# Gate tiles of a PEER layer: element scatters for two token tiles, one-hot products for the third, and each picked expert's U and V row fetched in one gather

## The reference, cut to what matters

```python
idx = jnp.take_along_axis(cand_i, pos, axis=-1)           # 8 heads x 16 experts a token
gates = jax.nn.softmax(top_s, axis=-1)
u = expert_u[ib]
act = jax.nn.gelu(jnp.einsum('td,thkd->thk', hb, u), approximate=False)
vv = expert_v[ib]
return jnp.einsum('thk,thkd->td', gb * act, vv)
```

## Time and the profile before

| | us |
|---|---|
| median of three runs | 1579.27 |
| runs | 1577.04 to 1581.59 |
| the profiled execution, its time | 1581.45 |
| its span | 1579.1 |
| PE busy | 1542.4 |
| DVE busy | 1263.5 |
| ACT busy | 717.6 |
| POOL busy | 343.5 |

### The profile page before, as it was taken

One profiled execution on the slowest core, in us unless ns is written; L12 is line 12 of the kernel. 1 busy time (PEld: TensorE's weight loads), 2 busy tenths in 40 slices (PEclk: granted clock), 3 DMA queues, 4 the chain that ended last, 5 costly groups with the idle time before them and its releaser, 6 DMA issues.

```text
span 1579.1 us, 23361 instructions
## 1 busy us (share of the span) xinstructions
PE 1542.4 (98%) x8161; PEld 1362.7 (86%) x8161; DVE 1263.5 (80%) x2625; ACT 717.6 (45%) x1128; POOL 343.5 (22%) x305
## 2 busy tenths in 40 slices
PE   7999998999999999999999999999999999999997
PEld 5786666789999999999999999988888888888886
DVE  6775655478988998898999999567888888888886
ACT  5424754443434343343667676434333333333333
POOL 0000003104122222222122222122333333333300
PEclk8999999999999999999999999999999999999999
DMA  9691021046878878789698998999999999999982
GB/s 361 237 366 64 1 107 57 0 174 259 286 247 283 294 235 277 252 291 295 230 319 299 339 321 300 355 326 319 361 348 356 355 351 361 348 360 351 353 284 103
DMA packets 177139, 427.38 MB, mean 271 GB/s; under 512 B 15072, under 2 KB 99200, under 8 KB 172416
## 3 DMA queue, kind: packets, MB, share of 16 engines
q1 hardware_dynamic: 140160, 291.67, 52.4%
q0 software_dynamic: 36864, 134.23, 24.2%
HBM read 373.42 MB, written 52.43 MB: 270 GB/s over the span
## 4 chain that ended last, share of the span: by engine, by line
PE 76%; DVE 1%; DMA 1%; ACT 0%; issue 0%; DVEq 0%; ACTq 0%
PE ps_y L1941 11%; PE ps_y L1945 11%; PE ps_y L1943 11%; PE ps_u L1153 11%; PE ps_u L1155 11%; PE ps_u L1154 11%; PE ps_g L1644 5%; PE ps_q L1320 2%; PE ps_q L1322 2%; PE ps_q L1321 2%; PE ps_s L1332 1%; DMA activations<-u_act 1%; PE ps_u L1976 0%; DVE y_scaled L1887 0%; DVE row L1908 0%
## 5 line engine op out<-in xcount | busy, mean ns | idle before, releaser
L1153 PE MATMUL ps_u<-h_hi,u_hi 128*128 128x384 f32 x1024 | 349.0, 341 | 1.2 <-ACT u_act L1163 0.9
L1155 PE MATMUL ps_u<-h_hi,u_lo 128*128 128x384 f32 x1024 | 344.9, 337 | 0.0
L1154 PE MATMUL ps_u<-h_lo,u_hi 128*128 128x384 f32 x1024 | 344.7, 337 | 0.0
L1812 ACT CAST v_hi<-v_raw 128x1024 fp32r<-128x1024 f32 x128 | 134.7, 1052 | 326.1 <-issue 320.9
L1212 POOL DMA_INDIRECT row<-in_v,row_index x128 | 173.2, 1353 | 376.7 <-DVE h_row L1232 320.4
L1212 POOL DMA_INDIRECT row<-in_u_rows,row_index x128 | 145.9, 1140 | 491.4 <-DVE row_dots L1219 404.7
L1870 DVE TENSOR_TENSOR v_lo<-v_raw,v_hi 128x1024 fp32r<-128x1024 f32 x128 | 160.4, 1253 | 101.3 <-ACT v_hi L1812 101.3
L1941 PE MATMUL ps_y<-v_hi,w_hi 128*128 128x512 f32 x768 | 237.9, 390 | 0.3 <-DVE w_lo L1857 0.3
L1945 PE MATMUL ps_y<-v_hi,w_lo 128*128 128x512 f32 x768 | 237.1, 389 | 0.0
L1943 PE MATMUL ps_y<-v_lo,w_hi 128*128 128x512 f32 x768 | 237.0, 389 | 0.0
L1143 DVE TENSOR_TENSOR u_lo<-u_raw,u_hi 128x1024 fp32r<-128x1024 f32 x128 | 155.0, 1217 | 69.3 <-ACT u_hi L1136 69.3
(11 more groups left out here) (302 smaller groups left out, 2236.0 us busy)
## 6 DMA issues: line engine op xcount, KB each, us to landing
u_raw<-in_u SPq DMA_DIRECT2D x128, 512.0 KB, 5.0
v_raw<-in_v SPq DMA_DIRECT2D x128, 512.0 KB, 5.7
activations<-u_act SPq DMA_DIRECT2D x128, 192.0 KB, 5.2
gate_tiles<-g_tile SPq DMA_DIRECT2D x12, 2048.0 KB, 9.1
gates<-gate_tiles SPq DMA_DIRECT2D x32, 768.0 KB, 8.2
act<-activations SPq DMA_DIRECT2D x128, 192.0 KB, 6.3
w_ada<-in_w_ada SPq DMA_DIRECT2D x23, 1024.0 KB, 7.7
w_proj<-in_w_proj SPq DMA_DIRECT2D x16, 512.0 KB, 4.7
```

What stands on the lines that cost most here:

```text
L1153: pe.matmul(out, self.hi[n][:, k], hi, start=(k == 0), stop=False)
L1154: pe.matmul(out, self.hi[n][:, k], lo, start=False, stop=False)
L1155: last = pe.matmul(out, self.lo[n][:, k], hi, start=False, stop=(k == KD - 1))
```

## The change

- `stick_breaking` also fills the part of `g_dram` of two dense tiles (8 tiles of 32 tokens, 16.8 MB) with zeros: four DMAs from one zeroed tile `blank`. `gated_linear` waits for them at its end.
- `mixer_back`: the eight `w_lo` go from POOL to DVE.
- `retrieval`: for the first two dense tiles ("loose") DVE works out, for each pick, its address in `g_dram` (`places_of`, `columns_of`, `jumps_of`, `cells_of`). As one expert can be picked by two heads, the gates of equal picks in earlier heads are added (`equal_picks`, `equal_gates`, `equal_sums`, `owe`: three operations over 512 g elements for head g, in turn g+1; `board` lies over the old `hits`). POOL then writes 32 scatters a head, each 128 elements of 4 bytes, 256 in all, at a pace written as block numbers (`SPREAD_AT`, `SPREAD_PACE`). Head 7's are prepared in `dense_gates`.
- `dense_gates`: one-hot products for the third tile alone, 16 batches, 37 blocks among them; three transposes for nine, and `product(80)` ahead of them.
- rows: one table of 2048 values (U row, V row), 128 gathers of 1 MB into a ring of four, for 256 of 0.5 MB into a ring of eight. For each pick dot, then Gelu and weight on ACT (one column each), and at the next pick the add. `ROW_PACE` spreads them: 30 by block 80, 68 by block 128 (61 by block 120), 128 by step 120 of V.
- `experts`: SP waits for all scatters before the first load of gates; two of the four activation buffers are now `up.act[0:2]`, so two loads come later.

```diff
+LOOSE_TILES = 2
+SPREADS = LOOSE_TILES * TOPK
-DOTS_BY = [0, 0, 8, 20, 32, 44, 56, 68, 81]
+ROW_PACE = [(16, 0), (80, 30), (128, 68), (248, PICKS)]
+SPREAD_AT, SPREAD_PACE = 13, 11.5
+def rows_by(b):
+    for (b0, n0), (b1, n1) in zip(ROW_PACE, ROW_PACE[1:]):
+        if b < b1:
+            return n0 + max(0, b - b0) * (n1 - n0) // (b1 - b0)
+    return PICKS
...
+            part = LOOSE * N_EXPERTS // P // FILLS
+            sp.wait_ge(blank_done, 1)
+            for n in range(FILLS):
+                sp.dma_start(flat[:, n * part:(n + 1) * part].rearrange("p (a n) -> p a n", n=D),
+                             blank[:].rearrange("p (o n) -> p o n", o=1).broadcast_to([P, part // D, D])).then_inc(keep["filled"], 16)
...
-                pool.tensor_tensor(w_lo[n % WS][:], keep["w_out"][:, n], w_hi[n % WS][:].bitcast(F32), ALU.subtract).then_inc(wlo, 1)
+                dve.tensor_tensor(w_lo[n % WS][:], keep["w_out"][:, n], w_hi[n % WS][:].bitcast(F32), ALU.subtract).then_inc(wlo, 1)
...
-    RING = 8
+    RING = 4
...
+    def weigh(self, act, q):
+        act.wait_ge(self.dotted, q + 1)
+        act.activation(self.act[:, q:q + 1], self.dots[:, q:q + 1], ACT.Gelu).then_inc(self.acted, 1)
+        act.wait_ge(self.acted, q + 1)
+        act.wait_ge(self.gated, q // TOPK + 1)
+        act.activation(self.weight[:, q:q + 1], self.act[:, q:q + 1], ACT.Identity, scale=self.gate[:, q:q + 1]).then_inc(self.weighed, 1)
+    def vector_at(self, dve, b, h_row):
+        for q in range(rows_by(b), rows_by(b + 1)):
+            self.dot(dve, q, h_row)
+            if q > 0:
+                self.add(dve, q - 1)
...
+    def equal_picks(self, dve, g, board):
+        mine = self.expert[:, 0:LOOSE_TILES, self.own(g)].rearrange("p b (k o) -> p b k o", o=1)                   .broadcast_to([P, LOOSE_TILES, TOPK, g * TOPK])
+        return dve.tensor_tensor(self.twin(g, board), mine, self.earlier(self.expert[:, 0:LOOSE_TILES], g), ALU.is_equal)
+    def equal_gates(self, dve, g, board):
+        return dve.tensor_tensor(self.twin(g, board), self.twin(g, board), self.earlier(self.gate[:, 1:1 + LOOSE_TILES], g), ALU.mult)
+    def equal_sums(self, dve, g, board):
+        return dve.tensor_reduce(self.twins[:], self.twin(g, board), AX.X, ALU.add)
...
+            q = 0
+            for g in range(PEER_HEADS):
+                for n in range(SPREADS):
+                    while q < PICKS and gather_at(q) < SPREAD_AT + SPREAD_PACE * (g + n / SPREADS):
+                        rows.gather(pool, q)
+                        q += 1
+                    spread_gate(pool, g, n)
...
+        def spread_gate(pool, g, n):
+            b, j = n // TOPK, g * TOPK + n % TOPK
+            if n == 0:
+                pool.wait_ge(picks.summed, g + 1)
+                if g > 0:
+                    pool.wait_ge(spread, 16 * SPREADS * g)
+            pool.indirect_dma_start(out=g_dram, out_offset=bass.IndirectOffsetOnAxis(ap=picks.cell[:, b, j:j + 1], axis=0),
+                                    in_=picks.owed[:, b, j:j + 1], in_offset=None).then_inc(spread, 16)
...
-        N_BATCH = DENSE // BATCH
+        N_BATCH = P // BATCH
...
+                    rows.vector_at(dve, b, h_row)
+                if x < PER_TILE:
+                    late_gates(2 * x)
+                    late_gates(2 * x + 1)
+                if x == PER_TILE - 1:
+                    dve.sem_inc(picks.summed, 1)
         def tensor(pe):
+            up.product(pe, FIRST)
             pe.wait_ge(chain, 4)
...
+            sp.wait_ge(spread, 16 * SPREADS * PEER_HEADS)
             load_gates(0)
```

More of the change, by code:

```diff
@@ L56 @@
 PICKS = PEER_HEADS * TOPK
+G_TOK = 32
+G_CELLS = N_EXPERTS * G_TOK
 ROW_TOK = P
@@ L1235, in retrieval @@
-def retrieval(nc, life, io, keep, picks, up, rows, h_row, query):
+        u = self.row[n][:, 0]
+        dve.tensor_tensor_reduce(u, u, h_row[:], 1.0, 0.0, ALU.mult, ALU.add, self.dots[:, q:q + 1]).then_inc(self.dotted, 1)
+    def weigh(self, act, q):
[4 more added lines that the diff above has]
+        act.activation(self.weight[:, q:q + 1], self.act[:, q:q + 1], ACT.Identity, scale=self.gate[:, q:q + 1]).then_inc(self.weighed, 1)
@@ L1239, in retrieval @@
+def retrieval(nc, life, io, keep, picks, up, rows, h_row, query, g_dram, spread):
     with ExitStack() as ctx:
@@ L1422, in beside @@
                         up.vector_at(dve, done[0])
+                        if done[0] == ROW_BLOCK[0]:
+                            dve.wait_ge(h_kept, 2)
+                        rows.vector_at(dve, done[0], h_row)
                         done[0] += 1
-                    while done[1] < DOTS_BY[h] + int(share * dots):
-                        if done[1] == 0:
-                            dve.wait_ge(h_kept, 2)
-                        rows.dot(dve, done[1], h_row)
-                        done[1] += 1
                 def settle(share):
@@ L1723, in experts @@
         over = lambda n: ctx.enter_context(nc.sbuf_tensor(n, [P, D], F32, side="right"))[:]
-        gate2, g_fin, squared = over("gate2_rows"), over("g_final_rows"), over("row_squares")
-        y_row, y_pair = h_row[:], [over(f"y_scaled{n}") for n in range(2)]
+        gate2, g_fin = over("gate2_rows"), over("g_final_rows")
+        y_row, squared, y_pair = rows.y[:], rows.row[0][:, 1], [rows.row[n][:, 1] for n in (1, 2)]
         total, rstd = sb("square_sums", [P, TB]), sb("rstd_rows", [P, TB])
@@ L1798, in sync @@
                 sp.wait_ge(o_done, b + 1)
-                sp.dma_start(io["out"][b], out_row[b][:]).then_inc(stored, 16)
+                sp.dma_start(io["out"][b], out_row[b]).then_inc(stored, 16)
             sp.wait_ge(stored, 16 * TB)
         def gpsimd(pool):
-            for r in range(PICKS + rows.RING, ROWS):
-                rows.gather(pool, r)
+            pass
         def scalar(act):
@@ L1832, in squares @@
                 act.activation(rstd[:, b:b + 1], total[:, b:b + 1], ACT.Exp, scale=-0.5).then_inc(rstd_done, 1)
-            act.wait_ge(rows.row_used, PICKS)
-            act.activation(rows.weight[:], rows.dots[:], ACT.Gelu).then_inc(rows.acted, 1)
             for i in range(-OPENING, N_KEYS):
@@ L1919, in vector @@
                     weigh(i + 2)
-                for r in adds_at(i):
-                    rows.add(dve, r, y_row)
+                rows.vector_at(dve, N_KEYS + i, h_row)
+                if N_KEYS + i == ROW_BLOCK[PICKS - 1] + 2:
+                    rows.add(dve, PICKS - 1)
                 if block_ok(i + 2):
```

313 lines of the change are left out of this document (197 added, 116 removed).

## The result

| | before | after |
|---|---|---|
| median, us (4 runs each) | 1579.53 | 1600.73 |
| range | 1577.04 to 1581.59 | 1598.53 to 1604.36 |
| span of the profiled execution | 1579.1 | 1596.7 |

The ratio is 1.0137, 95% interval 1.0110 to 1.0164: 1.4% slower, where 1531 (1515 to 1555) was forecast. In runs 4 and 5 two and one of the executions took over 1.5% longer than the fastest of the same kernel, and they are told apart there.

What follows compares the result with a forecast made beforehand. PE was taken to bound the kernel, with DVE the runner-up. Savings of 46.7 and 0.9 us, together 47.6, took the profiled 1581.45 to 1533.9; that execution lying 2.2 over the median, the forecast was 1531, range 1515 to 1555.

Steps and rivals of the forecast that it cites:

- What PE saves: Dense_gates: 32 of 48 one-hot batches go at 1.78 us, 57.0 us; fewer transposes, and the present wait and slow clock go.
- What DVE gets: Retrieval and dense_gates: equal-pick operations at 0.15 us + 1.04 ns an element; PE late by 14.7, leaving 46.7 us less.
- the signs: Expected marks of the new profile, among them a largest equal-pick operation of 3.7 us and PE waits of about 15 us.
- What feeds it: Retrieval and dense_gates: POOL instructions 1.24 us apart need 50.8 of 56.7 us; DMA share sums to 0.92.
- Rival 2: Late gathers: POOL falls behind, DVE waits for rows in dense_gates; some 10 us in each of two groups, 1551; chance 0.20.
- The two later activation loads: V stage: the loads have some 8 us to spare, so their cost is zero.
- Rival 3: Retrieval and dense_gates, blocks 13 to 105: scatter packets fill the DMA engines; +225 us, 1757, at 176 ns a packet; chance 0.10.
- The rule weighed with it: Scatters in retrieval and dense_gates: small writes done as read-modify-write, 19 us a turn, 40 us over the kernel, 1571.
- The mixer: Moving `w_lo` from POOL to DVE: 0.9 us less, with bounds of -3 (no clock drop) and +2.
- The fill: Stretch from 130 to 220 us: writing 16.8 MB of zeros costs zero, 0 to 5 us if stores are far slower.

Runs made afterwards that it cites:

- run 4: Changed kernel with no picked rows due in blocks 118 to 129: three executions from 1600.08 to 1607.14 us, two of 1627.52 and 1636.46.
- run 5: Changed kernel without the three wide operations on equal picks a head: three executions from 1612.76 to 1625.47 us, one of 1643.39.
- run 1: Changed kernel with one scatter in eight (32 of 256, the rest left out): 1548.40 us.
- run 12: Changed kernel with its 256 scatters turned into gathers (reads) of the same elements, low parts as in the changed kernel: 1593.28 us.
- run 3: Changed kernel with one loose tile instead of two (128 scatters, 32 batches of one-hot products): 1572.71 us.
- run 6: Changed kernel with one loose tile and no picked rows due in blocks 118 to 129: 1562.76 us.
- run 8: Changed kernel with low parts made by a one-input operation (raw x 0) instead of the two-input subtraction: 1643.68 us, a single execution.
- run 9: The kernel of run 8 with its 256 scatters turned into gathers (reads) of the same elements: 1565.92 us, two executions.
- run 13: Changed kernel with one loose tile (128 scatters) and low parts made by a one-input operation: 1561.48 us.
- run 2: Changed kernel with all 256 scatters, each of 16 partitions instead of 128: 1658.41 us.
- run 7: Changed kernel with a semaphore for each loose tile, so a head's first scatter waits only for the same tile's previous head: 1615.97 us.
- run 18: The kernel of run 17 with 26 rows instead of 30 by block 80 and 52 instead of 60 by block 118: 1570.73 us.
- run 17: Changed kernel with scatters paced over 13 blocks a head, no rows due in blocks 118 to 129, a semaphore for each loose tile: 1552.11 us.
- run 10: Changed kernel with the scatters' schedule started 5 blocks later (18 for 13), same pace: 1614.19 us.

## Why the prediction was wrong

By its own steps:

- **What PE saves** was right, as far as the runs show: a batch still takes 1.78 us. Run 1, the nearest to the change without its scatters, has 1548.4, and without the border's 11.6 it is within 6 of the forecast.
- **What DVE gets** was right in price: the largest equal-pick operations take 3.95 and 3.89 us for a forecast of 3.88 (0.15 + 3584 x 1.04 ns), and 12.3 us of waits where 14.7 were forecast, in the run in which POOL is out of the way. (The 3.7 among the signs does not follow from that sum.)
- **What feeds it** is the step that failed, in the term for POOL: "50.8 at 1.24, but 67.8 at the V gathers' mean of 1.35 + 0.3 ... I take 1.24, as scatters move few bytes." The 1.24 of the earlier trace rows are two gathers with DVE out of the way. Measured is 1.65, so 41 of them take 67.6 us where 56.7 are to be had: the upper bound of the sum, 67.8, was the right value. That the two agree so closely is luck, as the bound has 1.35 busy and 0.3 of issue, and the measured 1.65 is 1.27, 0.29 and 0.09 at the heads' borders, a wait that the sum left out. An instruction of POOL hardly depends on bytes (0.97 us for 128 elements of 4 bytes, 0.99 for a row gather of 1 MB). It is held while DVE works through operations of two inputs in SBUF, up to 8.44 us, and the value that the forecast chose has no room for it. The earlier trace rows had shown the two engines in each other's way, and it was used for the mixer only.
- **Rival 2** was the case that came. Its price failed as well: "some 10 us in each of two groups" supposes that POOL catches up. It can't while it is asked for 68 in 57: each head adds 11, and each gather waits behind them. Runs 12 and 1 put it at 45 us (1593.3 less 1548.4), with whatever 224 reads of 128 elements cost besides.
- **The two later activation loads** had "some 8 us to spare: zero". The border cost 11.2 us of PE (10 by runs 3 and 6). The room was counted for loads alone; the gate store, SP's wait and the stores behind it, all beside rows at 0.8 MB a block, use it up.
- **Rival 3**, packets that fill the DMA engines, did not come: from 687 to 950 us the DMA share is 0.74, for 0.87 in the same window of the kernel before. The sum had a packet for each element, 28 x 128 a turn (3584, not 3560) at 46 ns, a share of 0.19. The trace has sixteen packets a scatter, 448 a turn, at 13 ns, and sixteen more that signal the landing; by that the term was more than ten times too large, which did no harm. The writes cost 8 us in the changed kernel (run 12), in what form is not shown, and 78 in run 8, there as late instructions. The rule weighed with it (the Trainium skill, "DMA: Bandwidth & Descriptors", Specifications) would have had 40 us of it, as DMA time, which no run shows.
- **The mixer** was 0.9, measured 2.2 (0.6 to 3.6): the bound with no fall of the clock was the right one. The fill was zero, as forecast: from 130 to 220 us PE is as busy as in the earlier trace rows, with the DMA share at 0.50.

The sum, made again: 1531, with 45 more for POOL's time, 11 for the border, 8 for the writes, and 1.3 less for the mixer, is 1594; 7 of the 1600.7 stay unexplained. This is not a test of the 45 and the 8, which are differences of the same times; the 7 are what run 1 lies above the forecast with the border and the mixer in it, and its 32 scatters are a part of them.

The Trainium skill has the mechanism ("SBUF — State Buffer", Who interferes with whom): DVE and POOL share a read port, an operation with two inputs in SBUF holds it for its whole length, and an instruction of POOL that reads SBUF is blocked meanwhile, while a reduction never blocks. The traces agree on who is held and on the reduction (the next scatter took 0.97 us beside one), and they add when it ends: the 8.44 us last to the end of the dot, and the two-input add that comes next does not hold the scatter any more. Why it is let in there and at none of the ends before is not shown. The page infers in the same place that a two-input operation does not hold up descriptors; for indirect transfers, which read their indices from SBUF, the traces show that it does.

Not settled is the crawl. It needs writes (run 9 has none), and with 128 scatters there is next to nothing of it (none in run 13, 1.6 us on PE in run 6). It showed where POOL was freer (2, 5, 7, 8, 18), but also in the traced execution of run 4, where POOL was not; and it is absent in run 17, where POOL issues as many. Two of run 4's five executions were 20 us and more longer than the rest, and the one traced of these has it, so it may come and go between executions of one kernel; the others were not traced. Run 2 has it with sixteen elements a scatter, so bytes do not set it off. What does was not found.

## What to carry to other kernels

Ask of the engine that issues transfers what one asks of PE: how many instructions, at what mean distance, in what time. Take the distance from a stretch in which its neighbour works as it will after the change, not from the quietest row. If the demand is above the time, a later start or fewer barriers change little or harm (runs 10 and 7); the pace must be cut first (11.5 to 13 blocks), and then the same small edit pays (14.5 us for a semaphore). And a transfer moved to a border between stages must be counted with all that is queued there, stores too.

## What was not expected of the hardware

- An indirect transfer's instruction on POOL, 0.97 us alone, lasted 8.44 beside a chain of two-input operations on DVE, at the same place in two kernels with 256 and 32 scatters. It was let in at the end of one of them, and from there it took its 0.97 us, a further two-input operation beside it or not.
- 256 scatters of 128 elements of 4 bytes made PE's, DVE's and ACT's instructions issue late, matmuls 0.7 to 2.8 us apart for the most part, with the DMA engines at a share of 0.28 (516 to 520 us of run 8) and 0.02 (524 to 532): 78 us between runs 8 (one execution) and 9, which differ only in the direction of those transfers. Sixteen elements for 128 made it no better (61 us of issue time on PE); the packets are as many.
- A scatter of 128 elements of 4 bytes is sixteen packets of 32 bytes, 13 ns each, and not 128 packets.
